# Mixture-of-experts weights: 1 MiB chunks in 8 KB runs against host-packed 2 MiB pairs in 16 KB runs, in 24 slots

## The chip, the core and the metric

The kernel runs on one core of one Trainium2 chip. The metric is the device time of one execution in microseconds (us). Before the change the median of 3 runs is 1239.11 us (1237.75 to 1239.17).

## The reference

One decoder block on a sequence of 256 tokens with 1024 features, all in float32:

```
xn = RMSNorm(x)
u, q, k, v, q_idx, k_idx, w_idx, g_ssm, g_att = split(xn @ W_in)
y_ssm = GLU(gelu(S5(u)))                     # diagonal SSM, a scan over time
y_att = attention over the top 64 keys that an indexer chooses
x = x + (sigmoid(g_ssm) * (y_ssm @ P_ssm) + sigmoid(g_att) * (y_att @ P_att)) @ W_out
hf = RMSNorm(x);  gates = softmax of the top 4 of 32 router logits
for e in range(32):                          # the experts
    z = hf @ w_moe_in[e] + b_moe_in[e]       # 1024 -> 2048
    zg = min(z[:, ::2], 7);  zl = clip(z[:, 1::2], -7, 7)
    act = zg * sigmoid(1.702 * zg) * (zl + 1)
    out += gates[:, e] * (act @ w_moe_out[e] + b_moe_out[e])   # 1024 -> 1024
result = RMSNorm(x + out)
```

The experts' weights are 32 x (8 + 4) MiB = 384 MiB; each is read once from HBM.

## The kernel before

The first part of the program (the mixers) computes everything up to the residual x, with its own weights loaded in 27 chunks of at most 1 MiB through the four slots of `wbuf` (U, T, S, A, GLU, PS, PA and W chunks, in this order, `load` at L378). Each of these chunks consists of runs of about 1 KB or 2 KB. The second part is the loop over the 32 experts.

An expert's weights are 12 chunks of 1 MiB, each 128 partitions x 8 KB: chunks 0 to 7 are `w_moe_in`, 8 to 11 are `w_moe_out`. A slot holds one chunk. `ring` has 12 slots, which serve even experts. Nine more places (`extra`, L244: the four slots of `wbuf`, two pieces of `late`, and `mixed`, `x_t` and `x`) hold chunks 0 to 8 of odd experts. So chunks 0 to 8 have two places each, and chunks 9, 10 and 11 have only one, in the ring. The mixers' temporaries of the early part lie in `ring` too.

SyncE issues all of these loads in one written order. Expert 0's chunks and expert 1's first nine are issued during the mixers, each as soon as the buffer that lies in its place is done with (`load_first`, and the loop at L428). After that a chunk's load waits on `chunk_used`, a semaphore that TensorE raises once after the last matmul on each chunk (L1447, L1491): chunk n < 9 of expert e waits until expert e-2 has used its chunk n, and chunk n >= 9 waits until expert e-1 has. The order is written in two pieces. Up to expert `LEAD` = 6 the first nine chunks of expert e are issued ahead of the last three of e-1; then the last three of expert 6 and the twelve of expert 7 follow, and a loop issues each further expert's chunks in the order 0 to 11 (L443 to L455).

TensorE's work for an expert is `body` (L1425). The 64 token slots of the expert are the stationary operand, and two such 64-column halves work side by side. 8 chunks give the in-part (L1445) with a bias matmul behind chunk 0 (L1455). Then come the scatter of the expert before (L1420), the gather of the next (L1403), transposes (L1472, L1476, L1411), which wait for VectorE's activation (L1081 to L1087), and the out-part on the four `w_moe_out` chunks (L1488). In expert 31 there are also four matmuls for the output bias (L1463). The experts' sums stay in PSUM until the final RMSNorm.

Line numbers are those of the profile.

## Time and profile before

| | before |
|---|---|
| median of 3 runs | 1239.11 us (1237.75 to 1239.17) |
| the profiled execution | 1237.13 us |
| its span | 1235.3 us |
| TensorE busy | 1133.9 us, 92% of the span |
| VectorE, ScalarE, GpSimd busy | 358.2, 162.2, 92.0 us |
| DMA | 434.98 MB, 352 GB/s over the span |

The span is the time between the first and the last instruction of the profiled execution; 1.8 us lie around it. A busy share says how long an engine had something to do, not that the end depended on it. The DMA share is that of the core's 16 DMA engines together. The profile prints each TensorE fp32 matmul instruction twice, so "x8" stands for four matmuls, the work on one 1 MiB chunk.

### The profile page before, as it was taken

To read this page: it belongs to the slowest core of one execution; us is meant where nothing else is said; L and a number is where in the kernel's file an instruction comes from. 1 tells how busy PE (TensorE), PEld (TensorE's weight loads), DVE (VectorE), ACT (ScalarE), POOL (GpSimd) and SP (SyncE) were. 2 spreads that over 40 slices of the span, in tenths; PEclk is the share of its full clock that TensorE was granted. 3 is DMA by queue.
4 is the path that set the end of the run, shared out by engine and by line. 5 is a ranking of instruction groups with operands and counts; after the bars stand their busy time and mean duration, and the time that the engine had idled before them with its cause. 6 is when DMAs were issued, how large, how long until landed. Compare 5 with 4: busy or idle time off the path is not lost.

```text
span 1235.3 us, 14037 instructions
## 1 busy us (share of the span) xinstructions
PE 1133.9 (92%) x5406; PEld 490.8 (40%) x5406; DVE 358.2 (29%) x718; ACT 162.2 (13%) x307; POOL 92.0 (7%) x69
## 2 busy tenths in 40 slices
PE   7786769998999999999999999999999999999996
PEld 6774537886333333333333332323222323232322
DVE  4999947223111221111122121111111111111112
ACT  5001043413000010000000100000000000000002
POOL 4745610000000000000000000000000000000000
PEclk9988989999999999999999999999999999999999
DMA  7522342478999998999999999999999999999995
GB/s 218 176 68 72 133 170 102 141 306 315 391 426 422 427 376 365 424 427 423 427 423 427 423 427 422 427 423 426 423 426 423 426 424 425 424 425 424 425 424 209
DMA packets 89084, 434.98 MB, mean 352 GB/s; under 512 B 13528, under 2 KB 36384, under 8 KB 39904
## 3 DMA queue, kind: packets, MB, share of 16 engines
...
HBM read 433.52 MB, written 1.05 MB: 352 GB/s over the span
## 4 chain that ended last, share of the span: by engine, by line
PE 52%; DMA 19%; SPq 14%; DVE 9%; issue 4%; ACT 2%; POOL 1%; POOLq 0%; DVEq 0%
DMA ring<-in_w_moe_in 19%; PE ps L1445 17%; PE ps L1488 13%; SPq L440 12%; DVE ring L753 4%; PE ps L1420 3%; PE ps L1169 3%; PE ps L1403 3%; PE ps L1354 2%; DVE ring L882 2%; PE ps L1223 2%; PE ps L1472 1%; PE ps L1455 1%; PE ps L1344 1%; DVE late L915 1%
## 5 line engine op out<-in xcount | busy, mean ns | idle before, releaser
L1445 PE MATMUL ps<-ring,late 128*64 128x512 f32 x1024 | 234.0, 597 | 16.4 <-DMA ring<-in_w_moe_in 16.0
L1081 DVE TENSOR_SCALAR late<-ps 128x512 f32<-128x512 f32 x32 | 22.1, 692 | 707.6 <-PE ps L1445 707.6
L1488 PE MATMUL ps<-ring,late 128*64 128x512 f32 x896 | 198.5, 594 | 0.1
L1445 PEld LDWEIGHTS ps<-ring,late 128*64 128x64 f32 x1024 | 68.8, 136 | 177.2 <-issue 126.3
L1445 PE MATMUL ps<-wbuf,late 128*64 128x512 f32 x512 | 116.5, 596 | 0.0
L1488 PEld LDWEIGHTS ps<-ring,late 128*64 128x64 f32 x896 | 62.9, 137 | 122.6 <-issue 118.9
L716 ACT ACTIVATE late<-late 128x512 f32<-128x512 f32 x32 | 20.2, 630 | 530.7 <-DVE late L1081 530.7
L1169 PE MATMUL ps<-x_t,wbuf 128*128 128x256 f32 x320 | 70.9, 381 | 2.7 <-ACT ring L671 1.7
L1445 PEld LDWEIGHTS ps<-wbuf,late 128*64 128x64 f32 x512 | 35.2, 137 | 77.3 <-issue 75.0
L1169 PEld LDWEIGHTS ps<-x_t,wbuf 128*128 128x128 f32 x320 | 60.2, 190 | 12.4 <-issue 4.5
L1420 PE MATMUL ps<-late 64*128 64x512 f32 x256 | 63.6, 615 | 0.8 <-ACT late L723 0.8
L1403 PE MATMUL ps<-xs,late 128*64 128x512 f32 x256 | 61.9, 604 | 0.7 <-DVE late L753 0.7
L1223 PE MATMUL ps<-wbuf,x_t 128*128 128x221 f32 (+2 forms) x256 | 54.8, 378 | 0.0
L1223 PEld LDWEIGHTS ps<-wbuf,x_t 128*128 128x128 f32 x256 | 50.5, 201 | 4.8 <-issue 1.8
L723 ACT ACTIVATE late<-ps 128x512 f32<-128x512 f32 x32 | 19.1, 597 | 230.3 <-PE ps L1488 230.3
L753 DVE TENSOR_TENSOR late<-late 128x128 f32<-128x128 f32 (+3 forms) x104 | 40.2, 413 | 5.8
L753 DVE TENSOR_TENSOR ring<-ring 128x1024 f32<-128x1024 f32 (+1 forms) x26 | 36.5, 1452 | 12.9 <-ACT ring L681 12.6
L1420 PEld LDWEIGHTS ps<-late 64*128 64x128 f32 x256 | 22.1, 186 | 41.8 <-issue 41.8
L882 DVE TENSOR_TENSOR_SCAN ring<-par,ring 128x256 f32<-128x256 f32 x32 | 35.0, 1161 | 0.1
L1455 PE MATMUL ps<-u_in,late 32*64 32x512 f32 x256 | 34.8, 613 | 0.0
L1445 PE MATMUL ps<-x,late 128*64 128x512 f32 x128 | 30.6, 599 | 4.5 <-DMA x<-in_w_moe_in 4.5
L1445 PE MATMUL ps<-x_t,late 128*64 128x512 f32 x128 | 30.6, 599 | 4.5 <-DMA x_t<-in_w_moe_in 4.5
...
## 6 DMA issues: line engine op xcount, KB each, us to landing
ring<-in_w_moe_in SPq DMA_DIRECT2D x128, 1024.0 KB, 25.9
...
```

The lines of the kernel that those rows point to most:

```text
L440: sp.dma_start(dst, expert_chunk(e, n)).then_inc(done, 16)
L753: return ve.tensor_tensor(out_, a, b, op)
L882: ins = ve.tensor_tensor_scan(s[:, a, :], decay, s[:, a, :], 0.0, ALU.mult, ALU.add)
L1081: ve.tensor_scalar(gate_z, z[:, 0], LIMIT, None, ALU.min).then_inc(z_gate, 1)
L1169: i = pe.matmul(b[:, m * T:m * T + T], slot[:, k, (first_m + m) * P:(first_m + m + 1) * P], src[:, k, :], start=(k == 0), stop=(k == kt - 1))
L1223: i = pe.matmul(b[:, t * w:t * w + w], x_t[:, k, t * P:t * P + P], slot[:, k, :], start=(k == 0), stop=(k == KD - 1))
L1354: i = pe.matmul(ps[:, 4 + n, t * T:t * T + 256], mixed[:, k, t * P:t * P + P], slot[:, k, :], start=(k == 0), stop=(k == KD - 1))
L1403: i = pe.matmul(ps[64 * q:64 * q + SLOTS, 3, :], one_hot[:, t, :], xs[:, t, 512 * q:512 * q + 512], start=(t == 0), stop=(t == TT - 1))
L1420: i = pe.matmul(ps[:, 4 + 2 * t + q, :], gated_t[r, t * P:t * P + P], y_tok[r, :], start=False, stop=False, skip_group_check=True)
L1445: i = pe.matmul(ps[r, n // 2, :], h_sel[:, k % 4, k // 4, :], w[:, 512 * n:512 * n + 512], start=(k == 0), stop=(k == KD - 1))
L1455: pe.matmul(ps[r, n // 2, :], chosen[g, n, :], b_in[g, :], start=False, stop=False)
L1488: i = pe.matmul(ps[64 * q:64 * q + SLOTS, 2, :], act_tile(k), w[:, 512 * q:512 * q + 512], start=(k == 0), stop=(k == KF - 1))
```

## The change

The host packs the experts' weights into one tensor `w_moe`: per expert 6 parts of 2 MiB, each 128 partitions x 16 KB, contiguous for each partition. A part is what two chunks were, and is called a pair below; pairs 0 to 3 are `w_moe_in`, 4 and 5 are `w_moe_out`. One tensor `mem` has 24 slots of 8 KB per partition: pairs of even experts lie in slots 0 to 11, of odd ones in slots 12 to 23. All the mixers' buffers that were of their own or in `late` (x, x_t, mixed, u_in, wbuf and others) lie inside these slots. Room for this comes from smaller temporaries and a smaller scratch for dynamic DMAs (1024).

Each load of an expert pair waits for `chunk_used` of the expert two before it, and `chunk_used` counts pairs: six for an expert. The load of expert 0 and 1's pairs is spread over the mixers anew; the number given to `load_first` counts pairs of slots, 0 to 11. The experts' biases come packed, in one transfer early on. The last norm's gains are loaded behind the last weights as before. The order of the rows in `w_moe_out` within a chunk changes with the packing, and so the transposes of `act` read contiguous columns in place of every second.

```diff
-NX = 9
-LEAD = 6
+NSLOTS = 24
+SW = 2048
+CH = 2
+NT = 12 // CH
+NT_IN = 8 // CH
...
-        ring = sb("ring", [P, NW * SW])
+        mem = sb("mem", [P, NSLOTS * SW])
...
+        phase_re, phase_im = early(0, NCH, T), early(2 * SW, NCH, T)
+        state_re, state_im = early(4 * SW, 4, T), early(4 * SW + 1024, 4, T)
+        c_t = [early(5 * SW + 512 * n, 4, P) for n in range(2)]
+        u_in = early(5 * SW + 1024, KS, T)
+        prod = [early(6 * SW + n * 4 * T, 4, T) for n in range(4)]
+        o = 8 * SW
+        gate_s = early(10 * SW, KD, T)
+        k_t = early(11 * SW + MIX_TABLES, 2, T)
+        o2 = 11 * SW + MIX_TABLES + 512
+        par = early(o2, 24, NCH)
+        vec_rows = mem[0:72, o2 + 384:o2 + 512]
+        dt_rows = mem[0:NCH, o2 + 512:o2 + 640]
+        dt_pair = mem[0:NCH, o2 + 640:o2 + 642]
+        xs_re, xs_im = early(12 * SW, 4, T), early(12 * SW + 1024, 4, T)
+        b_nat = [early(12 * SW + 512 * n, 4, P) for n in range(2)]
+        c_nat = [early(12 * SW + 1024 + 512 * n, 4, P) for n in range(2)]
+        p_ssm = early(12 * SW, KD, T)
+        prod_out = [early(13 * SW + n * 4 * T, 4, T) for n in range(4)]
+        gate_a = early(13 * SW, KD, T)
+        y_ssm, y_att = early(14 * SW, KS, T), early(14 * SW + 1024, KS, T)
+        mixed = early(15 * SW, KD, T)
+        wbuf = mem[:, 18 * SW:22 * SW].rearrange("p (s n) -> p s n", n=SW)
+        x_t = early(22 * SW, KD, T)
+        x = early(23 * SW, TT, D)
...
-        b_in, b_out = [u_in[:, 2 * n:2 * n + 2, :].rearrange("p k t -> p (k t)") for n in range(2)]
-        vec_rows = sb("vec_rows", [72, P])
...
+        bias_rows = sb("bias_rows", [P, 1024])
+        b_in, b_out = bias_rows[:, 0:512], bias_rows[:, 512:1024]
...
-        act_rows = act.rearrange("p (b c i) -> p b i c", b=2, i=2)
+        act_t = gate_z.rearrange("p (j q s) -> p j q s", q=2, s=SLOTS)
...
-        moe_in = [sem(f"moe_in{n}") for n in range(NW)]
-        extra_in = [sem(f"extra_in{n}") for n in range(NX)]
-        b_in_in, b_out_in, gfin_in = sem("b_in_in"), sem("b_out_in"), sem("gfin_in")
+        moe_in = [[sem(f"moe_in{h}_{n}") for n in range(NT)] for h in range(2)]
+        bias_in, gfin_in = sem("bias_in"), sem("gfin_in")
...
-        def expert_chunk(e, c):
-            if c < NW_IN:
-                return io["w_moe_in"][bass.ds(e, 1), c * P:(c + 1) * P, :].rearrange("o p n -> p (o n)")
-            r = (c - NW_IN) * 2 * P
-            return io["w_moe_out"][bass.ds(e, 1), r:r + 2 * P, :].rearrange("o (p k) n -> p (o k) n", p=P)
-        def shaped(v, c):
-            return v if c < NW_IN else v.rearrange("p (k n) -> p k n", k=2)
-        def ring_slot(c):
-            return shaped(ring[:, c * SW:(c + 1) * SW], c)
-        def extra_place(c):
-            return shaped(extra[c], c)
+        def expert_part(e, n):
+            return io["w_moe"][bass.ds(e, 1), n].rearrange("o p n -> p (o n)")
+        def place_of(half, n):
+            return mem[:, (12 * half + CH * n) * SW:(12 * half + CH * n + CH) * SW]
...
+            sp.dma_start(bias_rows[:, :], io["moe_bias"]).then_inc(bias_in, 16)
+            def load_first(*pairs):
+                for p in pairs:
+                    for n in range(2 * p // CH, (2 * p + 2) // CH):
+                        half, at = n // NT, n % NT
+                        sp.dma_start(place_of(half, at), expert_part(half, at)).then_inc(moe_in[half][at], 16)
+            for name in CHUNKS[2:CHUNK["S2"]]:
                 load(name)
+            load_first(8)
+            for name in CHUNKS[CHUNK["S2"]:CHUNK["A3"]]:
+                load(name)
             sp.wait_ge(scanned, 8)
-            load_first((0, 1, 2, 3, 6))
+            load_first(0, 1)
+            sp.wait_ge(y_raw_ok, 1)
+            load_first(2)
             for name in CHUNKS[CHUNK["A3"]:CHUNK["W2"]]:
                 load(name)
             sp.wait_ge(rot_free, JOB["GLU1"] + 1)
             sp.wait_ge(y_ssm_ok, 1)
-            load_first((4, 5))
-            sp.wait_ge(att_done, 2)
-            sp.dma_start(extra_place(4), expert_chunk(1, 4)).then_inc(extra_in[4], 16)
+            load_first(3)
+            sp.wait_ge(row_max, 2)
+            load_first(4)
             load("W2")
             load("W3")
+            sp.wait_ge(gated_a, 1)
+            load_first(5)
             sp.wait_ge(mixed_ok, 4)
-            load_first(range(7, NW))
-            for n in range(4):
-                sp.dma_start(b_in[NE * n:NE * n + NE], io["b_moe_in"][:, 512 * n:512 * n + 512]).then_inc(b_in_in, 16)
-            for n in range(2):
-                sp.dma_start(b_out[NE * n:NE * n + NE], io["b_moe_out"][:, 512 * n:512 * n + 512]).then_inc(
-                    b_out_in, 16)
-            for n, done in ((0, (wout_done, 1)), (1, (wout_done, 2)), (2, (wout_done, 3)), (3, (wout_done, 4)),
-                            (5, (wout_done, 4)), (6, (rlogit, 1)), (8, (top_ok, 1)), (7, (sum_open, 1))):
-                sp.wait_ge(*done)
-                if n == 7:
-                    sp.wait_ge(x_norm, 2 * TT)
-                sp.dma_start(extra_place(n), expert_chunk(1, n)).then_inc(extra_in[n], 16)
+            load_first(6)
+            sp.wait_ge(wout_done, 3)
+            load_first(9)
+            sp.wait_ge(wout_done, 4)
+            load_first(7, 10)
+            sp.wait_ge(rlogit, 1)
+            sp.wait_ge(sum_open, 1)
+            sp.wait_ge(x_norm, 2 * TT)
+            load_first(11)
             def one_pass(c, first):
-                def load_chunk(e, n, odd):
-                    sp.wait_ge(chunk_used, (e + first - (2 if n < NX else 1)) * NW + n + 1)
-                    dst, done = (extra_place(n), extra_in[n]) if odd and n < NX else (ring_slot(n), moe_in[n])
-                    sp.dma_start(dst, expert_chunk(e, n)).then_inc(done, 16)
-                if isinstance(c, int):
-                    for e in range(2, LEAD + 1):
-                        for n in range(NX):
-                            load_chunk(e, n, e % 2)
-                        for n in range(NX, NW):
-                            load_chunk(e - 1, n, (e - 1) % 2)
-                    for n in range(NX, NW):
-                        load_chunk(LEAD, n, 0)
-                    for n in range(NW):
-                        load_chunk(LEAD + 1, n, 1)
-                with sp.Fori(LEAD // 2 + 1 if isinstance(c, int) else 0, NE // 2) as m:
-                    for odd in range(2):
-                        for n in range(NW):
-                            load_chunk(2 * m + odd, n, odd)
+                with sp.Fori(1 if isinstance(c, int) else 0, NE // 2) as m:
+                    for half in range(2):
+                        for n in range(NT):
+                            e = 2 * m + half
+                            if not isinstance(c, int) and half == 0 and n == 0:
+                                sp.wait_ge(gfin_in, 16 * c)
+                            sp.wait_ge(chunk_used, (e + first - 2) * NT + n + 1)
+                            sp.dma_start(place_of(half, n), expert_part(e, n)).then_inc(moe_in[half][n], 16)
+                sp.wait_ge(chunk_used, (first + NE - 2) * NT + 1)
+                sp.dma_start(gfin, io["norm_f_g"].unsqueeze(0).to_broadcast([P, D])).then_inc(gfin_in, 16)
             passes(sp, one_pass)
...
-                    ve.wait_ge(chunk_used, j * NW + NW_IN)
+                    ve.wait_ge(chunk_used, j * NT + NT_IN)
...
+                ve.wait_ge(gfin_in, 16 * c + 16)
                 ve.wait_ge(first_sum_ok, c + 1)
                 ve.tensor_copy(stat[:, 62:63], stat[:, 60:61])
             passes(ve, one_pass)
             ve.tensor_copy(stat[:, 63:64], stat[:, 60:61]).then_inc(tile_ok, 1)
-            ve.wait_ge(gfin_in, 16)
...
+                    def arrived(n):
+                        pe.wait_ge(moe_in[odd][n], 16 * pair + 16)
                     def weights(k):
-                        if k >= NX:
-                            pe.wait_ge(moe_in[k], 16 * j + 16)
-                        elif odd:
-                            pe.wait_ge(extra_in[k], 16 * pair + 16)
-                        else:
-                            pe.wait_ge(moe_in[k], 16 * pair + 16)
-                        return extra[k] if odd and k < NX else ring[:, k * SW:(k + 1) * SW]
+                        return mem[:, (12 * odd + k) * SW:(12 * odd + k + 1) * SW]
                     pe.wait_ge(h_sel_ok, j + 1)
                     if not head:
                         pe.wait_ge(gated_t_ok, j)
                     for k in range(KD):
+                        if k % CH == 0:
+                            arrived(k // CH)
                         w = weights(k)
                         for n in range(4):
                             r = slice(64 * (n % 2), 64 * (n % 2) + SLOTS)
                             i = pe.matmul(ps[r, n // 2, :], h_sel[:, k % 4, k // 4, :], w[:, 512 * n:512 * n + 512],
                                           start=(k == 0), stop=(k == KD - 1))
-                        i.then_inc(chunk_used, 1)
+                        if k % CH == CH - 1:
...
-                                pe.wait_ge(b_in_in, 16 * 4)
+                                pe.wait_ge(bias_in, 16)
...
-                        i = pe.transpose(ps[:, 0, n * P:n * P + P], act_rows[:, n // 2, n % 2, :], ident)
+                        i = pe.transpose(ps[:, 0, n * P:n * P + P], act[:, n * P:n * P + P], ident)
...
-                        c_ = NW_IN + k // 2
-                        if k % 2 == 0:
-                            two = weights(c_)
-                        w = two[:, (k % 2) * D:(k % 2) * D + D]
+                        if k % (2 * CH) == 0:
+                            arrived(NT_IN + k // (2 * CH))
+                        w = weights(KD + k // 2)[:, (k % 2) * D:(k % 2) * D + D]
...
-                        if k % 2:
+                        if k % (2 * CH) == 2 * CH - 1:
...
+def packed_experts(w_in, w_out):
+    into = w_in.reshape(NE, NT_IN, CH, P, 2 * F).transpose(0, 1, 3, 2, 4).reshape(NE, NT_IN, P, CH * SW)
+    out = w_out.reshape(NE, NT - NT_IN, 2 * CH, P, D).transpose(0, 1, 3, 2, 4).reshape(NE, NT - NT_IN, P, CH * SW)
+    return np.ascontiguousarray(np.concatenate([into, out], axis=1))
+def packed_biases(b_in, b_out):
+    rows = np.zeros((P, 1024), np.float32)
+    rows[:, 0:512] = b_in.reshape(NE, 4, 512).transpose(1, 0, 2).reshape(P, 512)
+    rows[0:2 * NE, 512:1024] = b_out.reshape(NE, 2, 512).transpose(1, 0, 2).reshape(2 * NE, 512)
+    return rows
...
-    nc = _bacc.Bacc("TRN2", target_bir_lowering=False, num_devices=1)
+    nc = _bacc.Bacc("TRN2", target_bir_lowering=False, num_devices=1, dynamic_dma_scratch_size=1024)
```

How the instructions move on SyncE while the mixers end. The names are destination<-source; `in_w_out` are the mixers' chunks W2 and W3, `ring`, `late` and `wbuf` are places of expert weights. Before:

```order
L401 DMA ring<-in_w_moe_in 128x2048 [waits y_ssm_ok,rot_free]
L401 DMA ring<-in_w_moe_in 128x2048
L415 DMA late<-in_w_moe_in 128x2048 [waits att_done]
L382 DMA wbuf<-in_w_out 128x8x256 [waits proj_done] x2
L401 DMA ring<-in_w_moe_in 128x2048 [waits mixed_ok]
L401 DMA ring<-in_w_moe_out 128x2048 x4
L423 DMA u_in<-in_b_moe_in 32x512 x4
L425 DMA u_in<-in_b_moe_out 32x512 x2
```

And now (L367 is the mixers' load, L390 the experts'):

```order
L390 DMA mem<-in_w_moe 128x4096 [waits y_ssm_ok,rot_free]
L390 DMA mem<-in_w_moe 128x4096 [waits row_max]
L367 DMA mem<-in_w_out 128x8x256 [waits proj_done] x2
L390 DMA mem<-in_w_moe 128x4096 [waits gated_a]
L390 DMA mem<-in_w_moe 128x4096 [waits mixed_ok]
```

In front of W2 and W3 stand two pairs (4 MiB) where three chunks (3 MiB) stood; behind them come 4 MiB where 5 MiB and six small bias loads came.

SyncE from W_out's matmuls on, to the start of the stream that waits for TensorE. Before:

```order
L433 DMA wbuf<-in_w_moe_in 128x2048 [waits wout_done] x4
L433 DMA mixed<-in_w_moe_in 128x2048 [waits wout_done]
L433 DMA x_t<-in_w_moe_in 128x2048 [waits rlogit]
L433 DMA late<-in_w_moe_out 128x2048 [waits top_ok]
L433 DMA x<-in_w_moe_in 128x2048 [waits x_norm,sum_open]
L440 DMA ring<-in_w_moe_in 128x2048 [waits chunk_used] x8
L440 DMA ring<-in_w_moe_out 128x2048 [waits chunk_used] x4
L440 DMA wbuf<-in_w_moe_in 128x2048 [waits chunk_used] x4
```

Now:

```order
L390 DMA mem<-in_w_moe 128x4096 [waits wout_done] x2
L390 DMA mem<-in_w_moe 128x4096
L390 DMA mem<-in_w_moe 128x4096 [waits x_norm,sum_open,rlogit]
L426 UNCONDITIONAL_BRANCH
L426 ISA
L433 ISA [waits chunk_used]
L433 DMA mem<-in_w_moe 128x4096
L432 REGISTER_ALU
L433 ISA [waits chunk_used]
L433 DMA mem<-in_w_moe 128x4096
```

The eight single chunks become four pairs, and the loop over experts starts at once with expert 2; there is no separate piece for the first experts, and no load that waits for the expert just before.

TensorE at the out-part of expert 0. Before (moe_in8 to moe_in11 are the arrivals of chunks 8 to 11):

```order
L1411 MATMUL ps<-table,late 128x128 x3
L1488 MATMUL ps<-ring,late 64x512 [waits moe_in8,act_t_ok]
L1488 MATMUL ps<-ring,late 64x512 x3
L1488 MATMUL ps<-ring,late 64x512 [waits moe_in9]
L1488 MATMUL ps<-ring,late 64x512 x3
L1488 MATMUL ps<-ring,late 64x512 [waits moe_in10]
L1488 MATMUL ps<-ring,late 64x512 x3
L1488 MATMUL ps<-ring,late 64x512 [waits moe_in11]
L1488 MATMUL ps<-ring,late 64x512 x3
```

Now (L1465 is the same line of work, L1390 was L1411):

```order
L1390 MATMUL ps<-table,late 128x128 x3
L1465 MATMUL ps<-mem,late 64x512 [waits moe_in0_4,act_t_ok]
L1465 MATMUL ps<-mem,late 64x512 x7
L1465 MATMUL ps<-mem,late 64x512 [waits moe_in0_5]
L1465 MATMUL ps<-mem,late 64x512 x7
```

The matmuls are the same; TensorE waits for two arrivals in place of four.

## Rows read from the trace of the kernel before

**Rows 1.** The page: DMA in 40 slices, and its packets.
```profile
DMA  7522342478999998999999999999999999999995
...
DMA packets 89084, 434.98 MB, mean 352 GB/s; under 512 B 13528, under 2 KB 36384, under 8 KB 39904
```

**Rows 2.** Chain that ended last: start us, us, what.
```profile
363.46 12.17 PE ps L1445 x56
...
390.60 12.17 PE ps L1445 x56
...
677.15 26.28 DMA ring<-in_w_moe_in
...
736.41 26.29 DMA ring<-in_w_moe_in
```

**Rows 3.** Windows: busy (x) of PE, PEld, DVE, ACT, POOL; clock, DMA share, GB/s.
```profile
24.00:30.00 6.00, 6.00 (x30) 5.28 (x29) 5.44 (x22) 3.60 (x7) 3.48 (x6) 1.00 0.98 323
...
700.00:1200.00 500.00, 472.39 (x2194) 149.97 (x2190) 84.70 (x203) 41.17 (x68) 0.00 (x0) 1.00 1.01 425
...
1232.00:1234.00 2.00, 0.00 (x0) 0.00 (x0) 0.00 (x0) 0.00 (x0) 0.00 (x0) 0.50 1.03 424
```

**Rows 4.** The same view, other windows.
```profile
309.00:311.00 2.00, 2.00 (x14) 0.49 (x8) 0.00 (x0) 0.00 (x0) 0.00 (x0) 1.00 0.51 127
...
450.00:500.00 50.00, 49.99 (x244) 17.06 (x242) 9.99 (x24) 4.84 (x8) 0.00 (x0) 1.00 0.87 359
...
1216.00:1218.00 2.00, 2.00 (x12) 0.72 (x10) 0.00 (x0) 0.00 (x0) 0.00 (x0) 1.00 0.57 225
```

**Rows 5.** Timeline of SyncE's DMA issues: start us, us, instruction.
```profile
301.57 0.33 SPq L433 DMA_DIRECT2D x<-in_w_moe_in  x1
308.78 13.51 SPq L440 DMA_DIRECT2D ring<-in_w_moe_in  x8
...
473.83 0.48 SPq L440 DMA_DIRECT2D late<-in_w_moe_out  x1
493.02 3.76 SPq L440 DMA_DIRECT2D ring<-in_w_moe_out  x3
```

**Rows 6.** Timeline of TensorE at expert 0.
```profile
306.80 1.94 PE L1445 MATMUL ps<-ring,late 128*64 128x512 f32 x8 [0.20 <-DVE late L753]
...
309.69 2.79 PE L1445 MATMUL ps<-ring,late 128*64 128x512 f32 x12
```

**Rows 7.** Timeline of SyncE's DMA issues in the mixers.
```profile
243.22 0.98 SPq L401 DMA_DIRECT2D ring<-in_w_moe_in  x2
...
255.99 7.29 SPq L382 DMA_DIRECT2D wbuf<-in_w_out  x2
```

**Rows 8.** Timeline of VectorE in the mixers.
```profile
215.49 2.29 DVE L948 TENSOR_REDUCE stat<-xs 128x8 f32<-128x2048 f32 x1
```

**Rows 9.** Timeline of TensorE in the mixers.
```profile
278.73 7.07 PE L1354 MATMUL ps<-wbuf,mixed 128*128 128x256 f32 x32
```

**Rows 10.** Timeline of TensorE, experts 30 and 31.
```profile
1179.39 1.99 PE L1420 MATMUL ps<-late 64*128 64x512 f32 x8
...
1184.61 7.09 PE L1488 MATMUL ps<-ring,late 128*64 128x512 f32 x32
1191.52 1.89 PE L1445 MATMUL ps<-wbuf,late 128*64 128x512 f32 x8
...
1211.18 1.99 PE L1420 MATMUL ps<-late 64*128 64x512 f32 x8
...
1215.53 1.94 PE L1488 MATMUL ps<-late 128*64 128x512 f32 x8
1217.29 5.32 PE L1488 MATMUL ps<-ring,late 128*64 128x512 f32 x24
```

**Rows 11.** Timeline of SyncE at the end of the stream.
```profile
1195.25 0.59 SPq L458 DMA_DIRECT2D ring<-in_norm_f_g  x1
```

**Rows 12.** The page's list of issues (last: us from issue to landing).
```profile
ring<-in_norm_f_g SPq DMA_DIRECT2D x1, 512.0 KB, 23.6
```

95 lines of the change are left out of this document (32 added, 63 removed).

## The prediction

> **What bounds the kernel now.** I read the page's slices first, then the chain of waits, then windows for the rates, and last the timelines at the places where the transfers pause.
>
> The page shows the 16 DMA engines at nine tenths or more from about slice 11 to the end, two slices excepted [rows 1]. The chain tells two regimes apart [rows 2]. Up to about 650 us it runs through TensorE, expert after expert, with a pitch of 390.60 - 363.46 = 27.14 us. From there it runs through the weights' loads: the same piece returns every 736.41 - 677.15 = 59.26 us for two experts (nine times in all), 29.63 us for one. Two experts are 24 MiB, so one MiB takes 59.26 / 24 = 2.469 us, 424.7 GB/s. Over 500 us in this regime the DMA share is 1.01 at 425 GB/s [rows 3]: the engines don't pause, the rate is what they can do with 8 KB runs.
>
> TensorE needs 27.14 us for an expert and the loads 29.63, so TensorE starts with loaded weights in hand, eats the lead up and then waits. The loads run flat out in both regimes. So the end is set by three things: when the loads begin to run without a pause, how many MiB are left then, and the time per MiB; behind the last MiB comes a tail. When the mixers end matters only through the first, TensorE's time per expert nearly not at all.
>
> The model applied to before: the first load that waits for TensorE is issued at 308.78 [rows 5], with 384 - 21 = 363 MiB left. The loads issued until 301.57 have drained by then: 309 to 311 us is busy by half [rows 4], so data flows again at about 310.1, 1.3 us behind the issue. 363 x 2.469 = 896.3. In 450 to 500 us the rate is 359 GB/s [rows 4]: (424.7 - 359) / 424.7 x 50 = 7.7 us of pause. It is the written order: at 473.83 SyncE had issued expert 7's first nine chunks, and the last three waited for expert 6's out-part until 493.02 [rows 5]. Sum 310.1 + 896.3 + 7.7 = 1214.1. The trace has the last weights at about 1216 (activity ends at 1216 + 0.57 x 2 = 1217.1 [rows 4], the last 1.2 us of it the 0.5 MiB of gains). The model is short by 2 us, which I leave in the range.
>
> **The change part by part, on the profiled execution's own time (span 1235.3, execution 1237.13, so 1.8 around it; the median of the runs shown is 2.0 above it).**
>
> *24 slots.* 24 MiB are issued ahead of the first wait on TensorE in place of 21: 360 MiB are left, 3 x 2.469 = 7.4 us less.
>
> *The pause at 450 to 500.* No load waits for the expert just before any more, and the second piece of the order is gone: -7.7. What could be late next is the start of the stream. TensorE frees a pair every 3.5 us in the in-part (7 chunks take 12.17 [rows 2]), then none until the out-part. Four pairs are 19.8 us of loading from about 313 on, until 333; the out-part takes the last 7.1 us of an expert's 27.14, so pair 4 is free at about 306.8 + 20.0 + 3.6 = 330.4, so no pause follows, and later the free slots only grow because TensorE is 2.5 us per expert faster.
>
> *Pairs as units, at the start.* Expert 2's first load waits for two chunks. The second chunk of expert 0 starts at 309.69 and takes 1.94 (as the first [rows 6]): free at 311.6, data from 311.6 + 1.3 = 312.9. Against 310.1 this is +2.8. W_out's third quarter ends at 278.73 + 7.07 = 285.8 [rows 9], its fourth at about 293: pair 9 goes at the first, 7 and 10 (4 MiB) at the second, drained at 293 + 1.3 + 9.9 = 304; pair 11 goes at about 301.6 (the conditions of [rows 5]'s first) and is drained at 309. The engines pause there for some 3.5 us; that is inside this term.
>
> *Earlier loads in the mixers.* Up to W2 two pairs (4 MiB) stand where 3 MiB stood. SyncE reaches them at 243.22 [rows 7]; their conditions are met (the row maxima of the second tile end at 215.49 + 2.29 [rows 8]). W1, issued just before, takes 3.2 us at the 1 KB runs' 323 GB/s [rows 3] and 4 MiB take 9.9, until about 258; W2 is issued at 255.99 [rows 7] and lands by 263. TensorE reads it from 278.73 [rows 9]: 15 us of cover, cost 0. If that cover were gone, the mixers would end later by the delay, 2 to 5 us, one for one. The pair in front of S2 and the bias transfer in front of T0 delay one chunk by 5 us and 1.2 us; the mixers have both behind VectorE's scan or within the reach of four slots. I take 0, at most 3. The six small bias loads go: 0.4 MB at that place, 1 us inside a stretch that pauses anyway.
>
> *The tail, counted from the end of the last weights' data, L.* Before: last out-part matmul ends at 1217.29 + 5.32 = 1222.6 [rows 10], 6.6 us behind 1216. A landing is seen about 1.7 us behind the end of its data (gains issued at 1195.25 [rows 11], 23.6 us to landing [rows 12], so 1218.85 against 1217.1). Now a pair takes 4.9 us. Expert 30's pair 3 is eight pairs ahead of L: seen at L - 37.3. Its two chunks 3.6, to L - 33.7. From in-part to out-part 1184.61 - 1179.39 = 5.2 us, the out-part 7.1 [rows 10], to L - 21.4; expert 31's in-part 1211.18 - (1184.61 + 7.09) = 19.5 [rows 10], to L - 1.9, its last pair being seen at L - 8.1; 1215.53 - 1211.18 = 4.4 to the out-part, and 7.1 for it: L + 9.6. The coarser pair costs 9.6 - 6.6 = 3.0 us. From there to the span's end 1235.3 - 1222.6 = 12.7, as now. Together L + 22.3.
>
> *16 KB runs.* No load of before has them, so the rate is bounded by the shorter runs [rows 3]. Per engine and packet: 1 KB runs at 323 GB/s and share 0.98, 16 x 1024 / (323 / 0.98) = 49.7 ns; 8 KB at 425 and 1.01, 16 x 8192 / 420.8 = 311.5 ns; the output's store has 4 KB at 424 and 1.03, 159.2 ns. A line through 1 and 8 KB gives 37.4 ns per KB and 610.7 ns for 16 KB, 2.0% more rate; one through 4 and 8 KB gives 38.1 and 616.2, 1.1% more. Between the two: 1.55%, 431.3 GB/s, 2.431 us per MiB. The ends: no gain at all (the fixed part of a packet is already nothing) or a small loss below, and 3% above, since the shares are rounded to a hundredth. TensorE's 27.14 us would ask for 463 GB/s.
>
> The Trainium skill ("DMA: Bandwidth & Descriptors", section "Where 436 GB/s comes from") gives a ceiling of 435.2 GB/s for the 16 engines together; this trace is below it at 425, and by it the time could not fall under about 1205 us.
>
> *Sum.* L = 312.9 + 360 x 2.431 = 312.9 + 875.2 = 1188.1. Span 1188.1 + 22.3 = 1210.4, execution 1212.2. The same model was 2 us short of before's end; with these the execution takes 1214, and I say 1214.
>
> As differences: slots and pause -15.1, the rate 360 x 0.038 = -13.7, the coarser pairs +2.8 and +3.0, in all -23.0, and 1237.13 - 23.0 = 1214.1. Other edits at nothing: TensorE's matmuls are the same (two arrivals waited for in place of four in the out-part); the transposes of `act` read contiguously, four short instructions per expert, of which the end sees only the last expert's; the wait for the gains moves ahead by one instruction of VectorE, while their load is issued as before behind the last weights and seen at about L + 3, before L + 9.6.
>
> **The rivals.**
>
> *The rate stays.* For it: at share 1.01 the engines are busy throughout, and the step from 4 to 8 KB runs gave only 2% (411.7 to 420.8), by rows whose shares are rounded and of which one is a store. Then L = 312.9 + 888.8 = 1201.7, span 1224.0, execution 1226; with a third of the gain 1221. The Trainium skill (same page, "Why small descriptors are slow (HBM only)") speaks against the change's longer runs: about three cycles per packet, against 256 beats of 32 bytes at 8 KB; by this estimate 16 KB brings 0.6%, which would make it some 1220.5 us. What this trace has at 1 KB against 8 KB is a bigger step than three cycles in 32 + 3, so it does not settle it.
>
> *The rate gains 2.5% or more.* 2.409 us per MiB: L = 1180, execution 1204. If the loads stopped being the bound, TensorE's own pitch would set the end: 306.8 + 31 x 27.14 = 1148.1 for expert 31's start, 1222.6 - 1191.7 = 30.9 and 12.7 behind it, execution 1193.5. Against: it takes 463 GB/s.
>
> *Slower: 16 KB runs are served worse than 8 KB runs* (each engine stays with one long read and one long write, and the 16 fall out of step). Place: all 360 MiB. It decides from L > 1235.3 - 22.3 = 1213.0, so above 2.500 us per MiB, below 419.4 GB/s, 1.25% less than now. At 415 GB/s L = 1222.5 and the execution takes 1246.6. Against: each step up in run length in this trace raised the rate.
>
> *The change doesn't do what it says: the mixers' end is pushed back* because pairs stand in front of mixers' chunks in the same queue. Each us of delay of expert 0 costs one. The cover on W2 is 15 us; for the others I have 3 to 5 us of possible delay: execution about 1218.
>
> **How the numbers follow.** Forecast 0.50 (its own range 1208 to 1219), rate stays 0.26 (1219 to 1228), rate up 2.5% or more 0.15 (1193 to 1207), mixers pushed back 0.04, slower 0.05. The range 1201 to 1228 leaves out most of the slower case and the lower half of the fast one, in all about 0.15 to 0.2. A measurement of this kernel tells 0.2% from no change: below 1236.6 counts as faster. Only the slower case reaches past it, with a sliver between: faster 0.94, within 0.01 to 0.02, slower 0.04.
>
> **What would show it.** The rate in windows after 700 us: 429 to 433 GB/s and the packets at 16 KB (24,576 fewer); the DMA engines without a pause between 313 us and the end; two experts every 58.3 us in the chain once the loads bound; the change of regime near expert 20 rather than expert 12; the first load that waits for TensorE issued at about 311.6; the last out-part matmul about 10 us behind the end of the weights. Wrong would be: a rate at or below 425, TensorE's expert 0 starting later than 307 us, or a new pause in the stream.

## The result, and the profile after

| | kernel before | changed kernel |
|---|---|---|
| median of the runs on the same chip | 1238.43 us (4 runs, 1237.72 to 1239.17) | 1219.32 us (4 runs, 1218.74 to 1220.73) |
| ratio to before, 95% interval | | 0.9847, 0.9831 to 0.9862 |
| profiled execution, its span | 1237.13, 1235.3 us | 1220.73, 1218.9 us |
| DMA packets | 89084 | 61290 |

The change makes the kernel 19 us faster. The forecast was 1214, 5 us too low: inside the stated range of 1201 to 1228, and 0.3 us above the 1208 to 1219 that was given to the forecast itself. The profiled execution of the changed kernel is the slowest of its four, that of before lies 1.3 us under its median, so the two profiles are 16.4 us apart and the medians 19.1.

The page of the changed kernel: its DMA slices, their rate, the packets, and the weights' loads (count, KB each, us from issue to landing):

```profile
span 1218.9 us, 13494 instructions
...
DMA  7633452386999999999999999999999999999993
GB/s 203 203 104 113 130 216 86 122 324 241 374 429 428 426 427 429 430 429 427 426 429 430 429 427 426 430 429 430 428 426 429 429 430 429 427 427 429 430 429 164
DMA packets 61290, 435.08 MB, mean 357 GB/s; under 512 B 10376, under 2 KB 33232, under 8 KB 36688
...
mem<-in_w_moe SPq DMA_DIRECT2D x192, 2048.0 KB, 42.5
```

From slice 11 to the last but one there is no dip any more; before had one, slice 16 [rows 1]. From slice 12 on the rate is 426 to 430. Packets of 8 KB and more fell from 49180 (89084 - 39904 [rows 1]) to 24602 (61290 - 36688), so by 24578, where the prediction had 24,576.

Windows of the changed kernel, with the columns of [rows 3] (busy of PE, PEld, DVE, ACT, POOL; clock, DMA share, GB/s):

```profile
311.00:313.00 2.00, 2.00 (x12) 0.63 (x10) 0.00 (x0) 0.00 (x0) 0.00 (x0) 1.00 0.16 66
313.00:315.00 2.00, 2.00 (x12) 0.72 (x10) 0.00 (x0) 0.00 (x0) 0.00 (x0) 1.00 0.60 123
...
300.00:350.00 50.00, 46.97 (x225) 16.49 (x223) 11.82 (x41) 7.29 (x11) 0.00 (x0) 1.00 0.94 396
350.00:400.00 50.00, 50.00 (x244) 17.15 (x244) 9.99 (x24) 4.80 (x8) 0.00 (x0) 1.00 1.01 428
...
450.00:500.00 50.00, 50.00 (x244) 16.93 (x240) 9.99 (x24) 4.80 (x8) 0.00 (x0) 1.00 1.00 426
...
700.00:1150.00 450.00, 429.08 (x2042) 141.41 (x2040) 79.92 (x192) 38.40 (x64) 0.00 (x0) 1.00 1.01 429
...
1194.00:1196.00 2.00, 2.00 (x10) 0.69 (x8) 1.17 (x2) 0.45 (x1) 0.00 (x0) 1.00 0.92 393
1196.00:1197.00 1.00, 0.70 (x4) 0.00 (x0) 0.93 (x3) 0.18 (x1) 0.00 (x0) 1.00 0.86 356
1197.00:1198.00 1.00, 0.38 (x3) 0.38 (x4) 0.97 (x3) 0.00 (x0) 0.00 (x0) 1.00 0.62 250
1198.00:1199.00 1.00, 0.72 (x7) 0.28 (x5) 0.49 (x2) 0.60 (x1) 0.00 (x0) 1.00 0.26 107
```

The reader is to see three things. In 450 to 500 us the share is 1.00 where [rows 4] had 0.87: the pause is gone. In the bound regime the rate is 429 where [rows 3] had 425: it rose, by less than forecast. And the stream ends over some 3 us instead of within one window of 2 us [rows 4]. Of the 3.6 us of DMA time that these four windows hold, 2.7 are used by 1197, and what is left is about the gains, so I put the end of the weights at about 1197.

The chain of waits of the changed kernel (start us, us, what):

```profile
392.01 12.17 PE ps L1423 x56
...
419.07 12.17 PE ps L1423 x56
...
770.85 12.17 PE ps L1423 x56
...
830.15 6.83 SPq L433
...
947.61 6.83 SPq L433
...
1065.07 6.83 SPq L433
...
1111.29 48.08 DMA mem<-in_w_moe
```

TensorE's pitch is 419.07 - 392.01 = 27.06 us, as before (27.14 [rows 2]). The chain stays with TensorE until expert 17 (392.01 is expert 3, and 392.01 + 14 x 27.06 = 770.85), where before it left TensorE at about 650 us, expert 12; the prediction said near 20. From there on it runs through SyncE's issues of loads, which now last 4.0 us or more each while the DMA engines are busy throughout; a single issue in the mixers lasted 0.33 us [rows 5]. The same piece returns after 1065.07 - 947.61 = 117.46 us, 24 pairs or 48 MiB (TensorE's four experts): 2.447 us per MiB, 428.5 GB/s, where the forecast had 2.431 and 431.3.

SyncE's DMA issues and TensorE at expert 0, then TensorE at expert 31, all of the changed kernel:

```profile
264.90 38.63 SPq L390 DMA_DIRECT2D mem<-in_w_moe  x6
...
313.41 26.88 SPq L433 DMA_DIRECT2D mem<-in_w_moe  x7
```

```profile
308.37 1.94 PE L1423 MATMUL ps<-mem,late 128*64 128x512 f32 x8 [0.20 <-DVE late L732]
310.24 1.09 PE L1434 MATMUL ps<-bias_rows,late 32*64 32x512 f32 x8
311.26 3.22 PE L1423 MATMUL ps<-mem,late 128*64 128x512 f32 x14
...
1187.69 7.09 PE L1423 MATMUL ps<-mem,late 128*64 128x512 f32 x32
1194.71 1.99 PE L1399 MATMUL ps<-late 64*128 64x512 f32 x8
...
1198.97 7.09 PE L1465 MATMUL ps<-mem,late 128*64 128x512 f32 x32
```

Expert 0 starts at 308.37 (before 306.80 [rows 6]), the first load that waits for it is issued 5.04 us behind that (before 1.98 [rows 5]), and the last out-part ends at 1206.06, 9 us behind the weights.

### The profile page after: what moved, and what is told of

It is laid out like the page before. It is cut to its first block, busy times and chain, and to the rows that moved or that the text cites. A ratio compares the mean times of both kernels' runs of the same rounds, so it can differ in the third digit from the quotient of the medians.

```text
span 1218.9 us, 13494 instructions
## 1 busy us (share of the span) xinstructions
PE 1125.7 (92%) x5406; PEld 494.4 (41%) x5406; DVE 358.4 (29%) x718; ACT 161.7 (13%) x307; POOL 92.3 (8%) x69
## 2 busy tenths in 40 slices
DMA packets 61290, 435.08 MB, mean 357 GB/s; under 512 B 10376, under 2 KB 33232, under 8 KB 36688
## 4 chain that ended last, share of the span: by engine, by line
PE 55%; SPq 25%; DVE 9%; DMA 4%; issue 3%; ACT 2%; POOL 0%; POOLq 0%; ACTq 0%; DVEq 0%
SPq L433 25%; PE ps L1423 22%; PE ps L1465 11%; PE ps L1148 4%; DMA mem<-in_w_moe 4%; DVE mem L732 4%; PE ps L1399 3%; PE ps L1382 3%; DVE mem L861 2%; PE ps L1333 2%; PE ps L1202 2%; PE ps L1434 2%; PE ps L1323 1%; DVE mem L894 1%; PE ps L1390 1%
## 5 line engine op out<-in xcount | busy, mean ns | idle before, releaser
L1423 PE MATMUL ps<-mem,late 128*64 128x512 f32 x2048 | 458.2, 595 | 23.0 <-DMA mem<-in_w_moe 22.8
L1423 PEld LDWEIGHTS ps<-mem,late 128*64 128x64 f32 x2048 | 141.6, 137 | 330.8 <-issue 282.3
L1465 PE MATMUL ps<-mem,late 128*64 128x512 f32 x1024 | 226.8, 595 | 0.0
L1465 PEld LDWEIGHTS ps<-mem,late 128*64 128x64 f32 x1024 | 70.7, 137 | 133.3 <-issue 128.1
L1148 PE MATMUL ps<-mem 128*128 128x256 f32 x416 | 93.2, 385 | 2.7 <-ACT mem L650 1.7
L1148 PEld LDWEIGHTS ps<-mem 128*128 128x128 f32 x416 | 79.6, 193 | 15.5 <-issue 4.7
L732 DVE TENSOR_TENSOR mem<-mem 128x16 f32<-128x16 f32 (+6 forms) x82 | 56.9, 725 | 16.3 <-ACT mem L660 12.6
L1202 PE MATMUL ps<-mem 128*128 128x221 f32 (+2 forms) x256 | 55.1, 379 | 0.0
L1202 PEld LDWEIGHTS ps<-mem 128*128 128x128 f32 x256 | 50.6, 201 | 5.0 <-issue 1.8
L702 ACT ACTIVATE late<-ps 128x512 f32<-128x512 f32 x32 | 19.1, 597 | 230.7 <-PE ps L1465 230.7
L732 DVE TENSOR_TENSOR late<-late 128x128 f32<-128x128 f32 (+2 forms) x99 | 38.6, 418 | 5.7
L861 DVE TENSOR_TENSOR_SCAN mem<-mem 128x256 f32<-128x256 f32 x32 | 37.0, 1224 | 0.1
L1434 PE MATMUL ps<-bias_rows,late 32*64 32x512 f32 x256 | 34.8, 613 | 0.0
L732 DVE TENSOR_TENSOR late<-ps,vec 128x512 f32<-128x512 f32 x32 | 22.1, 692 | 36.0 <-PE ps L1390 36.0
L1333 PE MATMUL ps<-mem 128*128 128x256 f32 x128 | 28.2, 380 | 1.5 <-DVE mem L732 1.5
## 6 DMA issues: line engine op xcount, KB each, us to landing
mem<-in_w_moe SPq DMA_DIRECT2D x192, 2048.0 KB, 42.5
```

Source lines behind the costliest of these rows:

```text
L732: return ve.tensor_tensor(out_, a, b, op)
L861: ins = ve.tensor_tensor_scan(s[:, a, :], decay, s[:, a, :], 0.0, ALU.mult, ALU.add)
L1148: i = pe.matmul(b[:, m * T:m * T + T], slot[:, k, (first_m + m) * P:(first_m + m + 1) * P], src[:, k, :], start=(k == 0), stop=(k == kt - 1))
L1202: i = pe.matmul(b[:, t * w:t * w + w], x_t[:, k, t * P:t * P + P], slot[:, k, :], start=(k == 0), stop=(k == KD - 1))
L1333: i = pe.matmul(ps[:, 4 + n, t * T:t * T + 256], mixed[:, k, t * P:t * P + P], slot[:, k, :], start=(k == 0), stop=(k == KD - 1))
L1423: i = pe.matmul(ps[r, n // 2, :], h_sel[:, k % 4, k // 4, :], w[:, 512 * n:512 * n + 512], start=(k == 0), stop=(k == KD - 1))
```

## The experiments

Twelve kernels. Each ratio is to the kernel before on the same chip, whose median there was 1238.15 to 1239.24 us, with its 95% interval.

### 1 and 2. Is it the length of the runs or the size of the transfers?

The changed kernel with single chunks of 1 MiB and 8 KB runs:

```diff
-CH = 2
+CH = 1
```

> The changed kernel with its transfers halved: 1 MiB with 8 KB runs, 24 slots and packing as they are. If the run length sets the rate, it falls from 428.5 back to 424.7 GB/s (2.469 us per MiB in place of 2.447, 360 x 0.022 = +7.9 us); the first slot is free 1.9 us earlier and the tail behind the last weights is 2 to 3 us shorter. In all some 3 us above the changed kernel's 1219.3: 1222 to 1224, ratio to before 0.987 to 0.989. If the rate gain came from anything else (one contiguous destination, the packed source), the rate stays at 428 and the time is 1215. Against before this run also prices the slots and the pause alone: forecast -15.1 in the prediction.

And with pairs of 2 MiB that consist of two 8 KB runs per partition:

```diff
-return io["w_moe"][bass.ds(e, 1), n].rearrange("o p n -> p (o n)")
+return io["w_moe"][bass.ds(e, 1), n].rearrange("o c p n -> p (o c) n")
...
-into = w_in.reshape(NE, NT_IN, CH, P, 2 * F).transpose(0, 1, 3, 2, 4).reshape(NE, NT_IN, P, CH * SW)
+into = w_in.reshape(NE, NT_IN, CH, P, SW)
```

> The changed kernel with 2 MiB transfers whose runs are 8 KB (two runs per partition, the source packed chunk by chunk). Run length sets the rate: 424.7 GB/s, +7.9 us, 1227, ratio 0.991. Rival, the size of a transfer sets it: rate 428.5, time 1219 as now, ratio 0.985.

Measured: 1229.36 us (0.9925, 0.9911 to 0.9938) for single chunks, 1232.19 (0.9954, 0.9940 to 0.9967) for pairs of 8 KB runs. The same window of the first and of the second:

```profile
500.00:1100.00 600.00, 579.89 (x2742) 188.99 (x2744) 104.89 (x252) 50.41 (x84) 0.00 (x0) 1.00 1.01 422
```

```profile
500.00:1100.00 600.00, 572.64 (x2726) 189.74 (x2726) 104.90 (x252) 50.43 (x84) 0.00 (x0) 1.00 1.01 422
```

Both run at 422 GB/s at full share, so at these slots the size of a transfer does nothing for the rate, and the length of its runs does. With 16 KB runs in the same slots the same kernel takes 1219.32: 12.9 us less than the second. But neither is at the 424.7 that the kernel before reaches with 8 KB runs. Something in the change costs rate, and the prediction had no such term. 422 GB/s is 2.485 us per MiB, 0.016 more than before's 2.469, and 360 x 0.016 = 5.8 us. With it the first kernel comes out: -7.4 - 7.7 + 5.8 = -9.3 against -8.8 measured.

The start of the stream, first kernel and second:

```profile
300.00:350.00 50.00, 46.97 (x225) 16.63 (x225) 11.75 (x41) 7.00 (x11) 0.00 (x0) 1.00 1.00 403
```

```profile
300.00:350.00 50.00, 46.97 (x225) 16.62 (x225) 11.76 (x41) 6.88 (x11) 0.00 (x0) 1.00 0.95 392
```

Against 422 GB/s these 50 us are short by 2.3 us with single chunks and by 3.6 with pairs. So pairs cost 1.3 us there, though their first waiting load is issued 2.8 us later (313.00 against 310.22): single chunks keep the engines at share 1.00 and still move only 403.

### 3. One pair issued later

```diff
+            sp.wait_ge(chunk_used, 1)
             load_first(11)
```

> The changed kernel, where the last of the 12 pairs issued ahead (slots 22 and 23) waits until TensorE has used its first pair. If the end is set by how many MiB are left when the stream begins to run without a pause, 2 MiB more are left: +4.9 us, 1224, ratio 0.9887. If the number of MiB loaded ahead does not matter so (the lead is eaten up anyway), 0: 1219.

Measured: 1224.14 us (0.9889, 0.9874 to 0.9904), 4.8 us above the changed kernel, against 2 x 2.447 = 4.9. In 300 to 350 us the share falls from 0.94 to 0.85 and nothing later gives it back:

```profile
300.00:350.00 50.00, 46.97 (x227) 16.61 (x227) 11.87 (x37) 6.50 (x10) 0.00 (x0) 1.00 0.85 356
```

So each MiB issued ahead of the first wait is worth its own loading time at the end, as the term for 24 slots said.

### 4. The output bias moved out of the last expert

```diff
-if tail and isinstance(c, int) and k < 2 * TT:
+if out_bias and isinstance(c, int) and k < 2 * TT:
```

with out_bias true for expert 1 only.

> The changed kernel with the four output-bias matmuls (some 1.05 us each) done in expert 1 and not in expert 31. Theory: the end hangs on a chain on TensorE from the arrival of expert 30's last in-part pair, L + 9 for the last out-part matmul; it gets 4.2 us shorter until the next chain (expert 31's last in-part pair, L + 7) takes over: -2 to -4 us, 1215 to 1217, ratio 0.982. Rival, the tail hangs on the last landing or on VectorE and ScalarE: 0.

Measured: 1219.99 us (0.9854, 0.9838 to 0.9869), no gain. Two things ate it. Expert 1 lasts longer and frees its slots later, while the stream has nothing in hand (windows: 417 GB/s where the changed kernel has 428), which is a loss of (428 - 417) / 428 x 50 = 1.3 us; the share stays at 1.00, so the engines do not stand still, and that the later slots are the reason is argued and not shown:

```profile
350.00:400.00 50.00, 50.00 (x244) 17.01 (x242) 9.99 (x24) 4.80 (x8) 0.00 (x0) 1.00 1.00 417
```

And expert 31, started sooner, now waits for its own last pair of the in-part:

```profile
1190.18 3.65 PE L1423 MATMUL ps<-mem,late 128*64 128x512 f32 x16 [1.25 <-DMA mem<-in_w_moe]
```

The prediction's tail had that pair seen at L - 8.1 and read from L - 5.5, 2.6 us ahead of its use; in the trace of after the 16 engines end up to 3 us apart, and a pair is whole only when the last of them is done.

The two profiles let the sum be followed further. The first waiting load goes at 311.90 in this run and at 313.41 in the changed kernel's, yet TensorE's next work behind expert 30's in-part starts at 1164.40 against 1162.99. So up to there this run lost 2.9 us, of which the window shows 1.3 and the rest I can't place. Expert 31 then gives back the 4.2 us of the bias and loses 0.61 and 1.25 to waits for its pairs: the last out-part ends at 1205.11 against 1206.06.

### 5. The loads alone

A kernel that only streams weights, ten stages of 48 MiB each, with 4, 8, 16, 32 and 64 KB runs, 1 or 2 MiB transfers, from the packed tensor and from the unpacked one, to low and to high slots. It computes nothing of the block; its output holds loaded data.

> Nothing but loads: ten stages of 48 MiB each, with no matmuls and no other engine (the block itself isn't computed; the output is filled with loaded data). Stages: runs of 4, 8 (1 MiB transfers), 8 (2 MiB transfers), 16, 32, 64 KB from the packed weights; 8 KB from the unpacked w_moe_in into the same slots; 8 KB packed into slots 12 to 23; 16 KB again; 8 KB unpacked into slots 12 to 23. If the run length alone sets the rate: 408 to 412, 422 to 425 (both transfer sizes), 428 to 431, about 432, about 433 GB/s, and source and slots make no difference. Rival: the 8 KB rate is 425 from the unpacked tensor and 422 from the packed one, or 425 in the low slots and 422 in the high ones; that would be where the changed kernel with 8 KB runs lost 0.6% of its rate.

Its page, rate in 40 slices, four slices a stage (one of the four dips where a stage drains; 4 KB runs; 8 KB in 1 MiB; 8 KB in 2 MiB; 16 KB; 32 KB; 64 KB; 8 KB unpacked; 8 KB in high slots; 16 KB; 8 KB unpacked in high slots):

```profile
GB/s 373 410 409 410 387 422 422 422 376 422 421 422 390 429 428 428 401 432 430 412 412 447 412 392 424 422 421 380 424 422 423 386 429 430 429 385 424 422 422 377
```

4 KB 410, 8 KB 422, 16 KB 428 to 430, 32 KB 430 to 432; the slices of 64 KB scatter too much to read. Source, transfer size and low or high slot change nothing. So 422 is the ordinary rate of 8 KB runs into such slots, and the question turns round: why did the kernel before have 424.7?

### 6 to 8. What the kernel before has that the changed one has not

```diff
-LEAD = 6
+LEAD = 10
```

> The kernel before with LEAD = 10 in place of 6: the switch to the plain order of loads comes four experts later, when TensorE has eaten 4 x 2.5 us more of the lead. Theory: the pause of 7.7 us at 450 to 500 us goes, nothing else changes: -7.7 us, 1230.5, ratio 0.9938. Rival: the pause is a fixed cost of the switch (or the loads ahead starve TensorE's out-part by then): 0 or slower.

Measured: 1232.63 us (0.9945, 0.9932 to 0.9959), 5.9 us less than before. The pause at 450 to 500 us is gone, and a smaller loss comes in its place:

```profile
450.00:500.00 50.00, 49.98 (x240) 17.11 (x240) 9.99 (x24) 4.84 (x8) 0.00 (x0) 1.00 1.01 425
...
550.00:700.00 150.00, 147.41 (x706) 49.25 (x704) 24.96 (x60) 12.70 (x21) 0.00 (x0) 1.00 1.01 420
```

The loss is 150 x 4.7 / 424.7 = 1.7 us at 550 to 700 us. It is the same change of order, now behind expert 10, as the packets there tell: those of expert 9's last chunk and expert 10's last three take 326 to 352 ns on average, where this kernel's fastest 8 KB packets take 309. This run also starts expert 0 at 308.34, though nothing ahead of it differs from before:

```profile
308.34 1.94 PE L1445 MATMUL ps<-ring,late 128*64 128x512 f32 x8 [0.20 <-DVE late L753]
```

The kernel before reading one packed tensor, chunk by chunk as it did:

```diff
-return io["w_moe_in"][bass.ds(e, 1), c * P:(c + 1) * P, :].rearrange("o p n -> p (o n)")
+return io["w_moe"][bass.ds(e, 1), c].rearrange("o p n -> p (o n)")
```

> The kernel before, reading the experts' weights from one tensor in which an expert's 12 MiB stand together (same 1 MiB chunks of 8 KB runs, same bytes, same places in the core's memory). If the source tensor is why 8 KB runs gave 422 GB/s in the changed kernel and 424.7 before: 422, +5.7 us, 1244, ratio 1.0046. Else 1238, ratio 1.000.

And the kernel before with a smaller DMA scratch area, which the change also alters:

```diff
-nc = _bacc.Bacc("TRN2", target_bir_lowering=False, num_devices=1)
+nc = _bacc.Bacc("TRN2", target_bir_lowering=False, num_devices=1, dynamic_dma_scratch_size=1024)
```

> The kernel before with the small scratch for dynamic DMAs (1024). If that is why the rate at 8 KB runs fell by 0.6%: 422 GB/s, 1244. Else, and this is the likelier, 1238 and 424.7 GB/s.

Measured: 1238.43 us (0.9997, 0.9988 to 1.0006) and 1238.86 (1.0004, 0.9995 to 1.0013), both at 425 GB/s. Neither is the cause. What is left that could touch every load is the destination. In the kernel before, nine of the 24 chunks of two experts go to places outside the ring. Two windows of its trace, inside one period of 59.26 us:

```profile
900.00:920.00 20.00, 18.50 (x88) 5.92 (x84) 4.99 (x12) 1.82 (x3) 0.00 (x0) 1.00 1.01 428
920.00:949.00 29.00, 27.19 (x130) 8.63 (x128) 4.99 (x12) 2.42 (x4) 0.00 (x0) 1.00 1.01 423
```

424.7 was a mean of two rates. `ring` is the first tensor in each partition, so its slots start at multiples of 8 KB, counted here and below from the start of the first tensor (where that lies itself no trace shows). Seven of the nine extra places stand behind `table`, which has 480 floats, and so 1920 bytes further; the two in `late` lie elsewhere again. (The expectations of experiments 9, 10 and 12 say 1408 bytes; that is the part of `table` which one of its two loads fills.)

The destination alone does not draw the border between the two rates. If only the nine chunks were fast, the mean would be (15 x 422 + 9 x 427) / 24 = 423.9. Windows of half a period, some 29.6 us from 890.0 on, read 427, 423, 427 and 422 GB/s in turn: 12 chunks are fast. The single packets say which. From expert 8 on the packets of even experts take 313.5 ns, and those of odd experts 309.0, the last three chunks included, which go to the same ring slots as those of even experts. Up to expert 6, where the order is another, it is the even experts' last three chunks that follow nine extra ones, and then they are the fast ones. So a load into a ring slot still has the fast rate when it comes right behind loads into the other places.

### 9. The loads alone, with shifted destinations

Twelve stages of 32 MiB, of which only the start of the destination differs. It too computes nothing of the block.

> Nothing but loads again (the block isn't computed), twelve stages of 32 MiB from the packed weights, in which only the place in a partition changes: 8 KB runs to slots that begin at a multiple of 8 KB plus 0, 64, 256, 1408, 4096 bytes; 16 KB runs plus 0, 64, 256, 1408, 4096, 8192 bytes; 4 KB runs plus 1408. Background: in the kernel before, 8 KB runs move at 421 GB/s into the ring (plus 0) and at 428 into the nine extra places (plus 1408 for most), which gives its mean of 424.7; all 24 slots of the changed kernel are at plus 0. Theory: the start of the destination sets it: 422 at plus 0, 428 at plus 1408, and for 16 KB runs 429 against 431 to 432. Rival: the place makes no difference when nothing else runs: 422 and 429 throughout.

Windows inside the stages: 8 KB runs shifted by 0, 256, 1408 and 4096 bytes, then 16 KB runs by 0, 256, 1408 and 8192, then 4 KB runs by 1408 (64 bytes read as 0 for both lengths, 16 KB by 4096 as by 8192). Rate in the last column:

```profile
20.00:70.00 50.00, 0.00 (x0) 1.00 1.01 422
...
184.00:234.00 50.00, 0.00 (x0) 1.00 1.01 422
266.00:316.00 50.00, 0.00 (x0) 1.00 1.01 427
348.00:398.00 50.00, 0.00 (x0) 1.00 1.01 422
430.00:480.00 50.00, 0.00 (x0) 1.00 1.01 429
...
594.00:644.00 50.00, 0.00 (x0) 1.00 1.01 429
676.00:726.00 50.00, 0.00 (x0) 1.00 1.01 432
...
840.00:890.00 50.00, 0.00 (x0) 1.00 1.01 430
922.00:972.00 50.00, 0.00 (x0) 1.00 1.03 422
```

1408 bytes lift 8 KB runs from 422 to 427, 16 KB runs from 429 to 432 and 4 KB runs from 410 (experiment 5) to 422. The other shifts do nothing, or 1 GB/s.

The packets of these windows show what kind of loss it is. With the shift nearly all take one and the same time (99% or more): 159 ns for 4 KB, 309 for 8 KB, 611 for 16 KB. Without it many take just that, and the others up to some 12 ns more: on average 313.6 ns for 8 KB and 614.2 for 16 KB, and 163.8 for 4 KB in experiment 5. The loss also needs time to set in: in the first stage, at shift 0, the packets still take 309 ns at 8 to 16 us, and 313.5 on average from 18 us on.

### 10 to 12. The slots shifted in the kernel

The changed kernel with `table` allocated in front of `mem`, so that the slots begin 1920 bytes behind a multiple of 8 KB (not 1408, as the expectation has it):

```diff
+        table = sb("table", [P, TB_END - MIX_TABLES])
         mem = sb("mem", [P, NSLOTS * SW])
...
-        table = sb("table", [P, TB_END - MIX_TABLES])
```

> The changed kernel with the small tensor of constants allocated in front of mem, so that each slot begins 1408 bytes behind a multiple of 8 KB. Theory (the destination's start matters, half as much per packet with 16 KB runs as with 8 KB): rate from 428.5 to 431.5 GB/s, 360 x 0.017 = -6 us, 1213, ratio 0.980. Rival (it doesn't, or only at 8 KB): 1219.3, ratio 0.985.

Measured: **1213.56 us** (5 runs, 1213.18 to 1214.56; 0.9798, 0.9785 to 0.9812), 5.8 us under the changed kernel and the fastest of all, together with the last one below.

```profile
500.00:1100.00 600.00, 585.42 (x2794) 194.98 (x2792) 107.31 (x256) 51.03 (x85) 0.00 (x0) 1.00 1.01 431
```

The same with single chunks (`CH = 1`) besides:

> The changed kernel with both edits: single chunks as transfers with 8 KB runs, and the slots 1408 bytes behind a multiple of 8 KB. If a destination's start and the run length each act by themselves, the rate is that of the loads alone with 8 KB runs at this start, 427 GB/s (2.456 us per MiB): 5 GB/s over the unshifted version with 8 KB runs (422, 1229.4), so 360 x (2.485 - 2.456) = 10.4 us less, 1218 to 1220, ratio 0.984. Then 8 KB runs shifted and 16 KB runs unshifted take the same time. If the run length is what counts and the start helps only 16 KB runs in the kernel, 1229. If 8 KB runs at this start are worth what 16 KB runs are (431), 1210.

Measured: 1218.19 us (0.9834, 0.9818 to 0.9851), at the rate of the loads alone:

```profile
500.00:1100.00 600.00, 586.10 (x2782) 192.21 (x2778) 104.83 (x252) 50.40 (x84) 0.00 (x0) 1.00 1.01 427
```

The changed kernel with `router` (1152 bytes) in front of `mem` and `table` where it was:

> The changed kernel with its slots 1152 bytes behind a multiple of 8 KB (the router's weights are allocated in front of them) in place of 1408 bytes. If any start that is far enough from a multiple of 4 KB helps, 431 GB/s and 1213 to 1215, ratio 0.980. If the gain hangs on this one distance, or on an odd multiple of 128 bytes within a KB (1152 = 1024 + 128, 1408 = 1024 + 384) the one or the other half of it: 1216 to 1219.3, where 1219.3 is the unshifted time and means no gain at all.

Measured: 1213.78 us (0.9804, 0.9788 to 0.9821), 431 GB/s: 1152 bytes do what 1920 do. In all three kernels the packets of 700 to 1150 us take one time, 309 ns for 8 KB (experiment 11) and 611 for 16 KB (10 and 12); without the shift they average 313.6 (experiment 1) and 614.7 (the changed kernel).

| median, us | slots at a multiple of 8 KB | slots 1920 bytes further |
|---|---|---|
| 1 MiB transfers, 8 KB runs | 1229.36 | 1218.19 |
| 2 MiB transfers, 16 KB runs | 1219.32 | 1213.56 |

Longer runs, with what the larger units cost, are worth 10 us at the one start and 4.6 us at the other; the shift is worth 11.2 and 5.8. The two overlap: with either of them the kernel is at 1218 to 1219. So at shifted slots most of the gain should be to be had without the host's packing, since packing the source alone did nothing (experiment 7); no kernel here was run that way.

## Why the prediction was right, and where its size was off

- **What bounds the kernel.** Right. The end is the time at which the stream becomes unbroken, plus the MiB left times the time of one, plus a tail. Experiments 1, 3, 10 and 11 each came out within 1 us of this sum once their rate was known, 6 once its smaller loss was counted.
- **24 slots, -7.4.** Right: 3 MiB at 2.47 us; taking 2 MiB away cost 4.8 of the 4.9 us it should (experiment 3).
- **The pause, -7.7.** Right: gone in the trace of after. In the kernel before, the order alone gave 5.9 us, since a smaller loss took part of it back; the change's own order has none (share 1.00 or 1.01 from 350 us on).
- **Pairs as units, +2.8 at the start and +3.0 in the tail.** Start: the first waiting load comes 5.04 us behind expert 0's start where before it came 1.98, +3.1 in place of +2.8. Tail: last out-part matmul at about L + 9.0, forecast L + 9.6. By whole kernels the pairs cost less: 1232.19 - 1229.36 = 2.8 us for both together, of the 5.8 summed. Half of the missing 3 us lies at the start, where the later issue costs 1.3 us of loading and not 2.8 (experiments 1 and 2). The other half I can't place: L itself is uncertain by 1 to 2 us where 16 engines end apart.
- **The mixers' earlier loads, 0.** Right. Expert 0 starts at 308.37, 1.6 us later than before's profile, and by "later than 307 us" the prediction would have called this wrong. It isn't the change: the kernel of experiment 6, which has the old mixers, starts it at 308.34, and that of experiment 10, which has the new ones, at 306.78. Over the traces of all kernels with the new mixers the start lies between 306.59 and 308.37, whatever differs behind it, and the profile of before had caught an early one.
- **16 KB runs, -13.7.** This is the mis-sized term. The step from 8 to 16 KB runs is just what was estimated: 422 to 428.5 GB/s at the same slots, 1.55% (forecast 1.55%), 12.9 us between experiment 2 and the changed kernel. But it starts from 422 and not from 424.7. Before's 424.7 was taken as the rate of 8 KB runs, and it was the mean over two rates, the faster of them started by loads into another sort of destination. The change puts all slots into one tensor at multiples of 8 KB, the slower sort, and that costs 5.8 us. Net -7.9. That the step fits the forecast to the hundredth is luck: it was the middle between 1.1% and 2.0%, and at shifted slots the same step is about 1% (427 to 431). There the changed kernel has the rate and the time that were forecast (431 GB/s, 1213.56 us, experiment 10), but 8 KB runs have 427 there too.

In medians: -15.1 for slots and order, +2.8 for the pairs, -7.9 for the rate, together -20.2 against -19.1 measured. The forecast's -23.0 differs from the measured one by +5.8 for the destinations, -3.0 for the pairs, and 1.1 not accounted for. It was also counted from a profiled execution 1.3 us under its median, which is that much of the 5 us by which 1214 was low.

**The rivals.** The rate did not stay, in the sense of that rival: it asked whether longer runs help, and they do. The time fell just inside this rival's range (1219 to 1228) all the same, since its numbers speak of the net rate (429 against 425). The Trainium skill ("DMA: Bandwidth & Descriptors", section "Why small descriptors are slow (HBM only)") has about three cycles per packet, by which the prediction's estimate made 0.6% of the step from 8 to 16 KB; at multiples of 8 KB the runs show 1.55%, and 2.9% from 4 to 8 KB. The measurement decides: there a packet costs more than that. At shifted slots both steps are about 1% (422, 427, 431 GB/s), nearer to it, so much of what longer runs save at multiples of 8 KB is no fixed cost of a packet but comes with the start of the slot. That the rival's 1220.5 us was nearer than 1214 is chance, the missing term being as large as the difference. Slower, 2.5% or more, and a push on the mixers did not come about.

**Not shown.** Why the start matters. 1152, 1408 and 1920 bytes help, 64, 256, 4096 and 8192 don't (or by 1 GB/s); all three that help are odd multiples of 128 bytes, but they are also the only starts between 256 and 4096, so sheer distance is not told apart from it, and no run here tried 128 or 1024. Nor is it shown why the loss takes some 16 us to set in and why ring slots escape it right behind shifted loads. Nor was it tried to issue only the first pair in halves, or only the last experts in single chunks; by experiments 1 and 2 both together would give some 3 us.
